# Zero products, transposes and branch layout on TensorE, ScalarE and VectorE in a three-stage transformer kernel

## What is computed

```python
# first block, h starts as x; mod = silu(c) @ w_ada + b_ada gives nine rows sh, sc, gt
h = h + 0.5 * gt1 * swiglu(modulate(rmsnorm(h), sh1, sc1))      # FFN 1, 2816 wide
h = h + gt2 * token_mixing(modulate(rmsnorm(h), sh2, sc2))      # pooling, dilated attention, gates
h = h + 0.5 * gt3 * swiglu(modulate(rmsnorm(h), sh3, sc3))      # FFN 2
x = rmsnorm(h)
# second block, two layers
mix = concat([retention, sliding_window_attention, latent_attention]) @ w_out
x = layer_norm(ALPHA * x + mix)
x = layer_norm(ALPHA * x + grouped_moe(x))                      # 16 experts, 2 of one group per token
```

## Time and profile before

| what | value |
|---|---|
| median of three runs | 1147.33 us (1146.07 to 1148.48) |
| time of the profiled execution | 1147.21 us |
| its span, first to last instruction | 1145.3 us |
| mean granted TensorE clock | 0.991 of full speed |
| busy: TensorE, VectorE, ScalarE, GpSimd | 96%, 77%, 55%, 8% of the span |
| chain that ended last | TensorE 76%, VectorE 14%, ScalarE 4% |
| moved by DMA | 271.95 MB, mean 237 GB/s |

### The profile page before, as it was taken

One profiled execution on the slowest core, in us unless ns is written; L12 is line 12 of the kernel. 1 busy time (PEld: TensorE's weight loads), 2 busy tenths in 40 slices (PEclk: granted clock), 3 DMA queues, 4 the chain that ended last, 5 costly groups with the idle time before them and its releaser, 6 DMA issues.

```text
span 1145.3 us, 25173 instructions
## 1 busy us (share of the span) xinstructions
PE 1100.7 (96%) x10834; PEld 844.5 (74%) x10834; DVE 882.6 (77%) x1112; ACT 631.1 (55%) x784; POOL 90.4 (8%) x104
## 2 busy tenths in 40 slices
PE   6999999999999999999999999999999999999996
PEld 5677776698788487777688785877759777596773
DVE  4789799788775885556667757999976775799994
ACT  1554444454456564344466445877856644677772
POOL 1114612061000110000000000000000000000000
PEclk9899999999999999999999999999999999999998
DMA  9999799565644587664555225599985322579981
GB/s 340 371 368 373 256 341 358 178 217 189 211 150 150 191 274 270 220 205 150 163 172 178 76 75 225 190 390 399 414 271 169 114 100 86 221 266 393 390 352 38
DMA packets 134718, 271.95 MB, mean 237 GB/s; under 512 B 9428, under 2 KB 98104, under 8 KB 126296
## 3 DMA queue, kind: packets, MB, share of 16 engines
q1 hardware_dynamic: 124248, 231.79, 57.1%
q0 software_dynamic: 7904, 29.25, 7.2%
q10 hardware_dynamic: 2464, 9.44, 2.2%
HBM read 269.41 MB, written 1.05 MB: 236 GB/s over the span
## 4 chain that ended last, share of the span: by engine, by line
PE 76%; DVE 14%; ACT 4%; issue 3%; DMA 3%; ACTq 0%; DVEq 0%; SPq 0%
PE ps L752 61%; DVE wlo L470 6%; DMA area<-in_w_ada_dram 2%; PE ps L1650 2%; PE ps L1698 1%; PE ps L894 1%; PE ps L1246 1%; PE ps L1276 1%; DVE area L2857 1%; PE ps L1286 1%; ACT whi L445 1%; DVE x L2277 1%; PE ps L1275 1%; DVE xn L2276 1%; ACT area L1801 1%
## 5 line engine op out<-in xcount | busy, mean ns | idle before, releaser
L470 DVE SCALAR_TENSOR_TENSOR wlo<-raw,whi 128x2048 f16<-128x2048 f32 (+2 forms) x214 | 470.6, 2231 | 36.1 <-ACT whi L445 35.2
L445 ACT ACTIVATE whi<-raw 128x2048 f16<-128x2048 f32 (+2 forms) x214 | 388.2, 1848 | 17.2 <-DMA raw<-in_w_ffn_in_dram 10.0
L752 PE MATMUL ps<-uhi,whi 128*128 128x256 f16 (+2 forms) x1328 | 329.5, 260 | 0.4 <-DVE ulo L2322 0.4
L752 PE MATMUL ps<-ulo,whi 128*128 128x256 f16 (+2 forms) x1328 | 329.2, 260 | 0.0
L752 PE MATMUL ps<-uhi,wlo 128*128 128x256 f16 (+2 forms) x1328 | 329.2, 260 | 0.0
L752 PE MATMUL ps<-whi,hreg 128*128 128x512 f16 (+1 forms) x672 | 210.7, 383 | 5.1 <-DVE area L2912 5.1
L752 PEld LDWEIGHTS ps<-area,whi 128*128 128x128 f16 (+2 forms) x2168 | 145.9, 99 | 12.8 <-issue 6.4
L752 PE MATMUL ps<-area,whi 128*128 128x96 f16 (+2 forms) x2168 | 155.3, 210 | 0.0
L752 PE MATMUL ps<-area,wlo 128*128 128x96 f16 (+2 forms) x1084 | 149.7, 210 | 0.0
L752 PEld LDWEIGHTS ps<-uhi,whi 128*128 128x128 f16 (+1 forms) x1328 | 130.2, 98 | 22.0 <-issue 7.4
L752 PEld LDWEIGHTS ps<-ulo,whi 128*128 128x128 f16 (+1 forms) x1328 | 130.1, 98 | 15.4 <-issue 1.9
(11 more groups left out here) (364 smaller groups left out, 1407.6 us busy)
## 6 DMA issues: line engine op xcount, KB each, us to landing
raw<-in_exp_w_gate_up_dram SPq DMA_DIRECT2D x64, 1024.0 KB, 7.7
raw<-in_w_ffn_in_dram SPq DMA_DIRECT2D x44, 1024.0 KB, 7.3
raw<-in_w_in_dram SPq DMA_DIRECT2D x34, 1024.0 KB, 6.7
area<-in_w_ada_dram POOLq DMA_DIRECT2D x48, 512.0 KB, 6.9
raw<-in_exp_w_down_dram SPq DMA_DIRECT2D x24, 1024.0 KB, 7.8
raw<-in_w_ffn_out_dram SPq DMA_DIRECT2D x22, 1024.0 KB, 7.7
raw<-in_w_out_dram SPq DMA_DIRECT2D x12, 1024.0 KB, 5.3
raw<-in_w_ada_dram ACTq DMA_DIRECT2D x4, 1024.0 KB, 9.6
```

The source lines that it names most:

```text
L445: act.activation(whi[:, u.slot, 0:n], raw[:, u.slot, 0:n], ACT.Copy, scale=SW)\
L470: dve.scalar_tensor_tensor(out=wlo[:, u.slot, 0:n], in0=raw[:, u.slot, 0:n], scalar=SW, in1=whi[:, u.slot, 0:n], op0=ALU.mult, op1=ALU.sub ...
L752: last = pe.matmul(o, st, mv, start=start and i == 0, stop=stop and i == 2, skip_group_check=True)
```

## The change

Five edits. (1) `last_downs` calls `between` six products later: behind the first half (n = 0) of v for tile 1, not ahead of v. This holds at all three places. (2) At the start five zero products are added behind `ada_direct(1, 2)` and five behind the last `ada_ones`. (3) The zero products that open FFN 1 go from six to five. (4) In `first_tile` the zero products go from eight to five. (5) On ScalarE and VectorE the condition is turned round: the slots version stands directly behind the branch, the dense one last, so that the branch falls through and the end of the slots version jumps over the dense one.

```diff
@@ -808,12 +808,12 @@
                                                 False, end and f == 1, weights_first=False)
                             if end and n == 0:
                                 last.then_inc(yh_done, 1)
+                                if t == TT - 1:
+                                    between()
                         if end:
                             last.then_inc(y_done, 1)
                         elif t == TT - 1:
                             last.then_inc(used, 1)
-                        if t == TT - 1 and not end:
-                            between()
@@ -851,7 +851,7 @@
                     open_y()
-                    for _ in range(6):
+                    for _ in range(5):
                         pe.matmul(ps[:, 3, :], ident16, zeros16[:, :], start=False, stop=False, skip_group_check=True)
@@ -1070,10 +1070,12 @@
             ada_direct(1, 2)
+            stay_warm(5, 1)
             pe.wait_ge(ada_sum, 12)
             ada_ones(1, range(4))
             pe.wait_ge(ada_sum, 13)
             ada_ones(1, range(4, 8)).then_inc(mod_mm, 1)
+            stay_warm(5, 1)
@@ -1216,7 +1218,7 @@
                 def first_tile():
-                    stay_warm(8, 7)
+                    stay_warm(5, 7)
                     token_transposes(1, 0)
@@ -2239,11 +2241,12 @@
-                with act.If(count > SLOTS):
-                    dense()
+                with act.If(count < SLOTS + 1):
+                    split_at[0] = ul + 24
+                    sparse()
                 with act.Else():
                     split_at[0] = ul + 24
-                    sparse()
+                    dense()
@@ -2945,11 +2948,12 @@
-                with dve.If(count > SLOTS):
-                    dense()
+                with dve.If(count < SLOTS + 1):
+                    split_at[0] = ul + 21
+                    sparse()
                 with dve.Else():
                     split_at[0] = ul + 21
-                    sparse()
+                    dense()
```

## The result

The changed kernel takes 1150.5 us (median of 8 runs, 1148.04 to 1151.47). The kernel before took 1148.19 us in 8 runs beside it, and 1147.1 to 1147.3 us in the later comparisons (29 to 32 runs each). The ratio on record is 1.0025, with a 95% interval from 1.0015 to 1.0034 (the two medians alone give 1.0020): slower by 0.25%, where I had forecast 1146.0 us and a range up to 1148.4. The profiled execution took 1151.18 us, its span is 1149.4 against 1145.3. One of the 32 later runs of the kernel before took 1623.79 us at a mean granted clock of 0.656, and no ratio uses it.

A forecast was written before the change was run, and what follows sets the result against it. TensorE, holding 76% of the chain, was taken as the bound. Start -1.75 and `between` +0.03, +0.18, +0.25, branches nothing, sum to -1.29 us on 1147.21: 1145.92, with the median 0.12 higher 1146.0 us; range 1143.8 to 1148.4.

The forecast's parts named there:

- The branches: ScalarE and VectorE: removing the taken branch counted as nothing, new end jump at 0.06 us covered, costing nothing.
- The rival that ended slower: End of slots version: VectorE's new jump waits for its code, statistics start late; 1151.5 us, chance 0.05.
- The sum of the rival: Late first statistics if VectorE's jump waits: 3.06 us in layer 0, 2.49 in layer 1, together 5.5 us.
- The start: Ahead of FFN 1: added zero products keep TensorE's clock up until `ulo` becomes the limit; gain 1.75 us.
- one case with a chance of 0.14 against it: Start: rival that the clock falls all the same, gain only 0.42 us, sum 1147.4 us; chance 0.14.
- `between`: Three calls: transposes of tile 0 behind six more products; costs 0.03, 0.18 and 0.25 us.
- the earlier end of tile 1's sums: All three `between` places: worth nothing, since VectorE is still in the split of tile 0 then.
- The sum: Whole kernel: -1.75 + 0.03 + 0.18 + 0.25 = -1.29 us, giving 1146.0 us.

The follow-up runs named there:

- e6: Kernel before with both swaps (ScalarE's and VectorE's branches turned round) and nothing else; 1151.44 us, ratio 1.0021 to 1.0046.
- e4: Changed kernel with ScalarE's never-run dense version of layer 0 cut from sixteen experts to four; 1145.88 us, ratio 0.9981 to 0.9999.
- e5: Changed kernel with VectorE's branch as before, ScalarE's still swapped; 1149.08 us, ratio 1.0007 to 1.0024.
- e8: Kernel before with only the start: ten added zero products and five for six behind; 1145.97 us, ratio 0.9972 to 0.9994.
- e3: Changed kernel with the branches of ScalarE and VectorE as before; 1145.75 us, ratio 0.9980 to 0.9998.
- e9: Kernel before with the start's added zero products spread more evenly, five for six in phase; 1146.60 us, ratio 0.9982 to 1.0000.
- e1: Kernel before with ScalarE's swap alone, slots version directly behind its branch, dense last; 1149.68 us, ratio 1.0016 to 1.0035.
- e2: Kernel before with VectorE's swap alone, slots version directly behind its branch, dense last; 1147.02 us, ratio 0.9987 to 1.0005.
- e7: Kernel before with `between` six products later at all three places and five zero products for eight; 1147.63 us, ratio 0.9993 to 1.0010.
- e10: Kernel before with only the five zero products ahead of `ada_ones` added; 1146.90 us, ratio 0.9985 to 1.0003.
- e11: Kernel before with only the five zero products behind `ada_ones` added; 1148.52 us, ratio 0.9997 to 1.0015.

## Why the prediction was wrong

**The step that failed** is in "The branches": "at 0.06 us it costs nothing either ... I take the row of the same two engines and the same distance". The term was 0 and measured 4.2 us (e6 against the kernel before; 2.4 to 5.3 by the interval). Three things were wrong in it. The record of a jump on ScalarE doesn't hold the wait for its target: it is 38 ns at a jump with 5.11 us of idle time behind it, whereas TensorE's record, 3.86 us long, does hold its wait, since the transposes start as it ends. The taken branch of the earlier trace rows did bring a transfer of code; three splits in the queue hid it, and the jump at the end has one piece of 0.59 us for cover. The trace of the kernel before showed both the transfer and the splits. And the same distance isn't the same price: it is the place of the target that counts, as layer 0, layer 1 and e4 show.

**The rival that ended slower** had the mechanism (the jump behind the slots version waits for its code), a chance of 0.05 and 1151.5 us, against 1150.5 measured. It named VectorE. The engine was ScalarE, whose place I had waved off with "a table load and a wait for VectorE in the same place": these cover 1.17 us, TensorE's own jump another 0.8, and the wait was 3.8 to 5.2. The sum of the rival, 5.5 us for two layers, was near by luck: what was measured is one layer's wait, and the half clock behind it.

**The start, -1.75 us.** Mechanism and limit were right: in the one profile in which the clock held (e5) the gain was 1.6 us, by the `ulo` pieces. Whether it holds was put as one case with a chance of 0.14 against it; it differs from run to run, as e8's mean clocks of 0.991 to 0.995 suggest. By the granted clock in the traces, the stretch at half clock at the start lasted 6.8 us in three of six kernels that have the ten products (e3 and the changed one) or nine of them spread (e9), 3.4 us in two (e4, e8) and there was none in one (e5). In the seven others (the kernel before, e1, e2, e6, e7, e10, e11) it lasted 6.8 to 10.2 us. The term measured -1.3 us in the median (e8; -3.2 to -0.7 by the interval).

**`between`, +0.46 us.** Measured +0.35 +- 0.9 by e7, and 0.19 by the trace of the changed kernel (it is 0.07 us ahead of the kernel before at the first place and 0.12 behind at the third). The transposes of tile 0 start as forecast: relative to VectorE's scaling ahead of them (line 2290), 0.25, 0.18 and 0.24 us later. TensorE's transposes of tile 1 (answers to the earlier trace rows):

```profile
233.13 1.06 PE L894 MATMUL ps<-small,xn 128*128 128x128 f32 x8 [0.68 <-DVE xn L2293]
```

```profile
401.27 1.09 PE L894 MATMUL ps<-small,xn 128*128 128x128 f32 x8 [1.25 <-DVE xn L2293]
```

```profile
582.14 1.06 PE L894 MATMUL ps<-small,xn 128*128 128x128 f32 x8 [1.08 <-DVE xn L2293]
```

They stand 0.01 us later, 0.07 earlier and 0.12 later than before. Two small things were missed. Eight transposes whose data is there take 1.04 us and not 1.09, so VectorE starts only 0.12 us later at the second place (393.38 against 393.26), where TensorE started 0.18 later. And VectorE's scaling of tile 1 there took 0.49 us where it took 0.67 before. That the earlier end of tile 1's sums is worth nothing held.

**The sum.** By the single edits: -1.3 + 0.35 + 4.2 = +3.2 us; the ratio of the changed kernel gives 1.7 to 3.9.

## What to carry to other kernels

A rarely used path that is put last isn't always free: on ScalarE here the jump over it was paid on the path that is used, at its end. Put that jump where the engine has some microseconds of cover, or leave the branch at the head, where here three splits were queued; and look for its price in the idle time behind it, not in its record. A jump that looks free in a trace may only be covered: look for a transfer of code behind it and for the work queued ahead of it. Two edits of one change can hide each other: without the swaps this change would have been a gain.

## What the runs showed of the hardware

- A jump's wait for code was 0, 1.91, 3.79, 4.38, 5.11 and 5.24 us on ScalarE, always the same line. On TensorE the record of the jump over its dense version of layer 0 varied as well, with code of the same length: 3.44 us (e11) to 5.30 (e8). In every kernel without a wait of ScalarE at this place the transposes start as that record ends, so TensorE's own jump is on the path there: 0.40 us (e11), 0.82 in the kernel before, 2.27 in e8 (850.1 + 5.30 = 855.4). How much of the scatter between runs comes from this and not from the clock, no run here tells. The transposes' row in e8:

```profile
855.46 1.27 PE L894 MATMUL ps<-small,xn 128*128 128x128 f32 x8 [2.44 <-issue]
```

- The length of an idle time doesn't tell whether a stretch at 1.2 GHz follows: behind TensorE's 2.84 us at the end of layer 0 the granted clock stayed at 1.00 (e1), behind 3.43 and 4.16 us it fell to 0.5 (e5, the change), but behind 2.44 us too (e8).
- The runs of the kernel before go with their mean clock: 62 runs at 0.990 to 0.991 have a median of 1147.0 us, 27 at 0.989 one of 1148.5 (the three later batches together; the two groups overlap by 1 us).
